# A two-block transformer kernel: a shorter lead and another rate for the filling of cross attention, and one subtraction moved down in the first MLP pair

## What is computed

```python
def cross_attention(h, mem_n, wq, wkv, wo):          # 4 heads of 256, 256 memory tokens
    q = (h @ wq).reshape(B, S, X_HEADS, X_HEAD_DIM)
    kv = (mem_n @ wkv).reshape(B, M, 2, X_HEADS, X_HEAD_DIM)
    s = jnp.einsum('bshd,bmhd->bhsm', q, kv[:, :, 0]).astype(jnp.float32) * X_HEAD_DIM ** -0.5
    p = jax.nn.softmax(s, axis=-1)
    o = jnp.einsum('bhsm,bmhd->bshd', p.astype(h.dtype), kv[:, :, 1]).reshape(B, S, D_MODEL)
    return o @ wo

def sq_relu_mlp(h, w1, w2):                          # 1024 -> 4096 -> 1024
    a = jax.nn.relu(h @ w1)
    return (a * a) @ w2
...
    h = h + cross_attention(rms_norm(h, norm_xattn_g[l]), mem_n, xattn_wq[l], xattn_wkv[l], xattn_wo[l])
    h = h + sq_relu_mlp(rms_norm(h, norm_mlp_g[l]), mlp_w1[l], mlp_w2[l])
```

## Time and profile before

| what | value |
|---|---|
| median of three runs | 2233.54 us (2231.29 to 2233.58) |
| the profiled execution | 2231.29 us |
| its span from first to last instruction | 2228.6 us |
| TensorE matmul busy | 2209.8 us, 99% of the span, 12112 matmuls |
| TensorE weight load busy | 1854.6 us, 83% |
| VectorE busy | 1454.6 us, 65% |
| ScalarE busy | 974.2 us, 44% |
| share of TensorE in the chain that ended last | 93% |
| granted TensorE clock | 0.999 of full speed |
| queries and attention of the second block's layer 0, from the lead on | 1092.5 to 1186.3 us |
| the same of layer 1 | 1769.4 to 1839.3 us |

### The profile page before, as it was taken

How to read it: one execution, slowest core, us unless ns; L and a number is a source line. 1 busy time by engine, 2 the same in 40 slices (tenths; PEclk the granted TensorE clock), 3 DMA queues, 4 the chain that set the end, 5 groups by cost and what they waited for, 6 DMA issues and landing times.

```text
span 2228.6 us, 31744 instructions
## 1 busy us (share of the span) xinstructions
PE 2209.8 (99%) x12112; PEld 1854.6 (83%) x12112; DVE 1454.6 (65%) x2448; ACT 974.2 (44%) x1676; POOL 14.5 (1%) x14
## 2 busy tenths in 40 slices
PE   9999999999999999999999999999999999999998
PEld 7777778888777788888898889998888888899997
DVE  5866555557656566586765777776755656776775
ACT  5444443334445344364554544443322434444444
POOL 0000000000000000200000000000000000000000
PEclk9999999999999999999999999999999999999999
DMA  5655443335645333455354333333233313233331
GB/s 200 187 159 163 136 132 106 106 122 173 179 140 162 112 95 116 131 162 151 109 148 145 101 95 95 105 100 100 95 95 95 95 48 100 90 105 95 97 113 55
DMA packets 136694, 268.14 MB, mean 120 GB/s; under 512 B 21773, under 2 KB 79931, under 8 KB 136160
## 3 DMA queue, kind: packets, MB, share of 16 engines
q1 hardware_dynamic: 136544, 266.13, 39.1%
HBM read 235.37 MB, written 26.77 MB: 118 GB/s over the span
## 4 chain that ended last, share of the span: by engine, by line
PE 93%; DVE 2%; ACT 1%; issue 1%; DMA 1%; POOL 0%; SPq 0%; DVEq 0%; POOLq 0%; ACTq 0%
PE ps L2064 29%; PE ps L2066 29%; PE ps L2065 29%; PE ps L2081 2%; PE ps L2092 2%; ACT t_Tb L2288 1%; POOL t_UP L2047 0%; DVE t_wlo L2380 0%; PE ps L2116 0%; PE ps L2106 0%; PE ps L2104 0%; PE ps L2105 0%; PE ps L2118 0%; PE ps L2117 0%; DVE t_UP L2640 0%
## 5 line engine op out<-in xcount | busy, mean ns | idle before, releaser
L2064 PE MATMUL ps<-t_P0H,t_whi 128*128 128x512 f32 (+1 forms) x1568 | 592.6, 378 | 2.2 <-DVE t_P0L L2425 1.6
L2065 PE MATMUL ps<-t_P0L,t_whi 128*128 128x512 f32 (+1 forms) x1568 | 584.6, 373 | 0.0
L2066 PE MATMUL ps<-t_P0H,t_wlo 128*128 128x512 f32 (+1 forms) x1464 | 552.7, 378 | 0.0
L2380 DVE TENSOR_TENSOR t_wlo<-t_raw,t_whi 128x1024 fp32r<-128x1024 f32 (+2 forms) x289 | 342.6, 1186 | 38.6 <-PE ps L2066 26.4
L2207 ACT ACTIVATE t_whi<-t_raw 128x1024 fp32r<-128x1024 f32 (+2 forms) x295 | 300.7, 1024 | 152.4 <-PE ps L2066 149.8
L2064 PEld LDWEIGHTS ps<-t_P0H,t_whi 128*128 128x128 f32 x1568 | 295.2, 188 | 79.0 <-issue 23.3
L2065 PEld LDWEIGHTS ps<-t_P0L,t_whi 128*128 128x128 f32 x1568 | 295.0, 188 | 55.4 <-issue 1.0
L2066 PEld LDWEIGHTS ps<-t_P0H,t_wlo 128*128 128x128 f32 x1464 | 275.2, 188 | 54.7
L2064 PE MATMUL ps<-t_P1H,t_whi 128*128 128x512 f32 (+1 forms) x548 | 210.1, 383 | 2.2 <-DVE t_P1L L2765 1.0
L2065 PE MATMUL ps<-t_P1L,t_whi 128*128 128x512 f32 (+1 forms) x548 | 208.4, 380 | 0.0
L2066 PE MATMUL ps<-t_P1H,t_wlo 128*128 128x512 f32 (+1 forms) x524 | 201.1, 384 | 0.0
(11 more groups left out here) (341 smaller groups left out, 3883.0 us busy)
## 6 DMA issues: line engine op xcount, KB each, us to landing
t_raw<-in_wts SPq DMA_DIRECT2D x362, 512.0 KB, 3.6
far<-t_Tb SPq DMA_DIRECT2D x26, 384.0 KB, 3.0
far<-t_Tb SPq DMA_DIRECT2D x16, 512.0 KB, 3.1
t_PTX<-far SPq DMA_DIRECT2D x64, 96.0 KB, 3.0
t_raw<-in_wts SPq DMA_DIRECT2D x16, 384.0 KB, 3.0
t_QKV<-far SPq DMA_DIRECT2D x32, 128.0 KB, 3.3
t_raw<-in_wts SPq DMA_DIRECT2D x13, 256.0 KB, 3.1
t_PTX<-far SPq DMA_DIRECT2D x24, 128.0 KB, 4.0
```

Source lines behind the costliest of these rows:

```text
L2064: e.matmul(s.out, s.sh, s.mh, start=s.first, stop=False, skip_group_check=again)
L2065: e.matmul(s.out, s.sh, s.ml, start=False, stop=False, skip_group_check=again)
L2066: i = e.matmul(s.out, s.sl, s.mh, start=False, stop=s.end, skip_group_check=again)
L2380: e.tensor_tensor(s.dst, s.raw, s.hi.bitcast(F32), ALU.subtract).then_inc(*mark("lo", s.j))
```

## The change

Both calls of `drive` in `cross` take 2 turns of `fill` ahead of the first stage where they took 6. The rate of layer 1 goes from 25/6 (4.167) turns for each stage to 13/3 (4.333). In the first MLP pair of each layer (`n == 2`), the subtraction of `w1`, with the fetch behind it, goes from the place behind `other(0)` to the place behind `low(n + 1, "u1", 0)`, just ahead of `other(2)`.

```diff
         if l == 0:
-            drive(main(), fill(), 5, 1, lead=6)
+            drive(main(), fill(), 5, 1, lead=2)
         else:
-            drive(main(), fill(), 25, 6, lead=6)
+            drive(main(), fill(), 13, 3, lead=2)
...
             c11 = add(a0, z, s1, p)
             PB.give(bz, c11)
             other(0)
-            if n == 2:
-                low(n, "w1", 3)
             if more:
                 u0(n + 1)
...
             s3 = snap(b1, p)
             c22 = add(b1, v, s3, p7)
             low(n + 1, "u1", 0)
+            if n == 2:
+                low(n, "w1", 3)
             other(2)
             low(n + 1, "w0", 2)
```

## The result

| | before | after |
|---|---|---|
| median | 2233.22 us of 4 runs (2231.29 to 2233.58) | 2250.57 us of 4 runs (2250.26 to 2251.81) |
| profiled execution, its span | 2231.29, 2228.6 us | 2252.59, 2249.8 us |
| granted TensorE clock, mean | 0.999 | 0.996 |
| matmul busy | 2209.8 us | 2217.7 us |

The change makes the kernel slower: the ratio of the times is 1.0084, with a 95% interval of 1.007 to 1.0097, or 17.35 us on the medians. The forecast was 13.56 us, so the direction is right and the size is not: 2250.57 lies just above the upper end of the range. Six further executions of the kernel after, the profiled one among them, took 2251.33 to 2253.45 us, so the four of the median are on the low side.

The account below looks back on a forecast made before the run. TensorE's own matmul stream was taken as the bound, so each new wait is paid in full: 1.68 + 1.69 + 1.30 + 2.02 - 0.70 + 0.51 + 7.06 = 13.56 us, forecast 2246 us, range 2240 to 2250.5.

Parts of the forecast that it names:

- The waits of attention: Cross attention: first scores 1.68 and 1.69 us, layer 1 units 2 and 4 1.30 and 2.02, layer 0 values 0.51.
- The aside: Layer 1, units 2 and 4: waits 1.15 us less each, 0.2 and 0.9, if the weight's subtraction is appended elsewhere.
- The rate: Layer 1's cross attention: one more filling group shortens the wait on output subtraction L2765, -0.70 us.
- The moved subtraction: First MLP pair of both layers: other(2) waits for w1's subtraction in a serial chain, 3.53 us each, 7.06 us together.
- the fetch behind it costs nothing: First MLP pairs: the fetch is issued some 8 us later, but its weight is rounded only behind other(3); no cost.
- The sum: All terms added: 13.56 us, giving 2244.85 on the profiled execution and 2247.10 on the median; 2246 was taken.
- this case: Rival: the clock falls in the two gaps ahead of other(2), 2250.4 to 2252.6 us; chance 0.04.
- all else in the trace is at full clock: Argument against the clock falling in the two gaps: the rest of the trace before the change shows full clock.
- The rival's price: Clock falling to 1.2 GHz for other(2) in both layers: its 2.77 us doubled, 5.5 us together; chance 0.04.
- The base: Starting time for the sum: profiled execution 2231.29 us, the fastest of three runs, or the median 2.25 us above it.

Follow-up runs that it names:

- the run with the filled gaps: Only the subtraction of w1 moved against the kernel before, plus twelve useless matmuls in the gap ahead of each first other(2): 2239.80 us, ratio 1.003.
- the other pair of runs: Only the subtraction of w1 moved against the kernel before, without and with twelve useless matmuls in each gap: 2243.46 us and 2239.80 us.
- both gaps at half: Only w1's subtraction moved against the kernel before, but placed ahead of the next u1's subtraction: 2238.94 us, ratio 1.0027.

## Why the prediction was right about the waits and wrong about the time

**The waits of attention.** All came where they were forecast, and within 0.1 us: 1.78, 1.78, 1.39, 2.07 and 0.51 against 1.68, 1.69, 1.30, 2.02 and 0.51. The forecast had the slower start of the first matmul in it, which these distances leave out, so the true costs are 0.08 more. What was too small is the delay: all four scores start 0.26 us after their subtraction ends and not 0.05 (1097.60 to 1097.86 at the first), and I can't say why. The aside that the waits at units 2 and 4 would be 1.15 less if the weight's subtraction stood elsewhere was wrong: it left out ScalarE's rounding.

**The rate.** The wait on L2765 went from 1.18 to 0.44, as forecast (0.70 less).

**The moved subtraction.** 3.45 us each, 3.52 with the slower start, against 3.53. The snap starts 0.04 us after the product's last matmul ends (1311.63 + 0.28, 1311.95), so ScalarE's rounding no longer holds it up, as I had chosen. That the fetch behind it costs nothing holds too, since the run with the filled gaps costs no more than the gaps.

**The step that failed: the clock.** The sum had no term for it: all matmuls were taken to run at full clock behind the new gaps. Measured, the waits sum to 1.78 + 0.51 + 1.78 + 1.39 + 2.07 - 0.74 + 3.45 + 3.45 = 13.7 us, 14.4 by the table with all that hangs on them; forecast 13.56. To this come two falls of the clock, one behind each gap, at 1.6 us each by the table (1.4 to 1.8 by the other pair of runs): 3.2, and so 17.6 against the 17.35 of the medians, whose interval is 15.6 to 21.7. I gave this case a chance of 0.04. For it there was a rule of the Trainium skill, named below; against it I held, one wait of 2.0 us with the clock at 1.00 behind it. This was a weak witness twice over: the wait is shorter than the new gaps, as the prediction itself says, and it was one execution of something that goes either way. And "all else in the trace is at full clock" was a misreading: the same trace is at half clock from about 2223.7 us on. In the fourteen profiles here the clock fell

| behind waits of | falls | of |
|---|---|---|
| 3.45 us and more (both gaps in two kernels, and 3.82 ahead of unit 6) | 5 | 5 |
| 2.31 and 2.39 us (both gaps at half) | 1 | 2 |
| 2.14 us (the old wait, 2.0 in the lists of waits, unfilled in 12 profiles) | 8 | 12 |
| 2.06 to 2.1 us (unit 4) | 2 | 5 |
| 1.78 us (the first scores) | 0 | 10 |

In three of the five in the first row the clock fell just before the wait ended. The table leaves out the program's start, where one profile has a fall at a wait of 2.1 us near 7.5 us, and its end, where all fourteen have one, four of them already at the wait of 1.3 us. So the length of the wait isn't all that sorts them. Ahead of the old wait, as ahead of that last one, stand eight matmuls of one column each, where groups of 512 columns stand ahead of the scores of units 2 and 4; whether that matters no run here shows. The old wait in the kernel before:

```profile
1020.56 1.02 PE L2135 MATMUL ps<-t_ones,t_TMP 128*128 128x1 f32 x8 [0.24 <-ACT t_TMP L2239]
1023.58 0.35 PE L2064 MATMUL ps<-t_MH,t_whi 128*128 128x256 f32 x1 [2.00 <-DVE t_wlo L2380]
```

The rival's price was off as well, in the other direction: I took that all twelve matmuls of `other(2)` run at half speed, 2.77 us more each. Only 3.4 us pass at half clock, in which eight of them start, so it is 1.6 each. That the measured time lies inside this rival's 2250.4 to 2252.6 is therefore luck in part: on the base of the profiled execution, a price 2.3 us too high for the two falls made up for waits 0.8 too low and a base 1.9 below the median.

**The rule that pointed the right way.** The Trainium skill, "TensorE: Matmul & The Clock Gate", section "Why this matters for your kernels", warns against idle gaps longer than about 3 us between bursts of matmuls. The two gaps of 3.45 us agree with it. The traces go further: falls came behind waits of 2.07 to 2.31 us too, in a part of the executions.

**The base.** The profiled execution of before had no fall behind its old wait and others have one, which is 1.4 us where profile and median are 1.9 apart. The sum on the median was 2247.10; the 2246 that I gave split the difference for no reason. So of the 4.57 us between 2246 and 2250.57 some 0.8 are the base, 0.8 the waits and 3.2 the clock, which is 0.2 more than there is to explain.

**What stays open.** Why the clock falls behind the same wait in one execution and not in the next, why the scores start 0.26 us behind their subtraction, and what makes the start of the program differ by up to 1 us.

## What to carry to other kernels

Where TensorE is the bound, a gap has two prices: its length, and the slow stretch that may follow it. At all five waits of 3.45 us and more the second was paid here (1.6 us for each gap of the whole change), so it belonged in the sum and not among the rivals; for shorter waits look at several executions, and at what TensorE does ahead of the wait, before you say what the clock does. Where the gap can't be avoided, matmuls of no use in it take the second price away. And before moving a piece of work on a strictly ordered engine, write down what stands idle beside it now: `w1` was free at its old place, and the weight's subtraction ahead of `query_lo` was nearly free too.

## What the hardware showed that I had not expected

In these profiles the clock stays at half for 3.4 us after such a wait (6.8 us in two of them, behind the old wait), and matmuls then follow each other 0.43 us apart and not 0.23 for 512 columns. Behind waits of 2.06 to 2.4 us it fell 11 times of 19 in all, and behind the old wait it did in one execution of the kernel before and not in the other. Adding 24 matmuls of no use made a kernel 3.66 us faster.
